# A decoder trunk whose MLP takes its up panels in pairs: seven half products in place of eight, on two thirds of the tokens

## What is computed

```
h2 = (rmsnorm(x, g_norm2[l]) * (1.0 + sc2) + sh2).astype(x.dtype)
ff = jnp.square(jax.nn.relu(h2 @ w_up[l])) @ w_down[l]
x = (x + g2 * ff).astype(x.dtype)
```

## Time and profile before

| what | before |
|---|---|
| median of 3 runs | 2797.01 us |
| lowest and highest | 2795.2 and 2807.06 us |
| profiled execution, first to last instruction | 2801.3 us |
| PE, PEld busy | 97%, 90% |
| DVE, ACT, POOL busy | 44%, 23%, 9% |
| DMA | 295 MB, mean 105 GB/s |

### The profile page before, as it was taken

The page is one execution under the profiler, slowest core; times in us unless marked ns, Lnnn a source line. Parts: engine busy times, 40 slices in busy tenths (PEclk is TensorE's granted clock), DMA queues, the critical chain, the costliest instruction groups (busy, mean ns, idle before and its releaser), DMA issues. The chain is left out here.

```text
span 2801.3 us, 48407 instructions
## 1 busy us (share of the span) xinstructions
PE 2711.2 (97%) x20524; PEld 2531.6 (90%) x20524; DVE 1234.9 (44%) x2205; ACT 644.0 (23%) x1058; POOL 263.6 (9%) x344
## 2 busy tenths in 40 slices
PE   5999989999999999999999999899999999999998
PEld 4999976699999999999989999666999999999998
DVE  5625535557423423324457354456563243242344
ACT  4334324423101101001132442343221000000012
POOL 1101100020000000001111110001100000000010
PEclk9999999999999999999999999899999999999999
DMA  8440159731222221111134101895212111111111
GB/s 310 151 108 31 67 211 328 265 115 40 82 91 85 82 91 58 56 46 46 61 112 118 51 31 62 296 347 214 75 49 79 46 46 50 42 59 46 46 55 69
DMA packets 106873, 295.37 MB, mean 105 GB/s; under 512 B 19605, under 2 KB 32790, under 8 KB 104610
## 3 DMA queue, kind: packets, MB, share of 16 engines
q1 hardware_dynamic: 106498, 291.49, 30.6%
q0 software_dynamic: 160, 0.79, 0.1%
HBM read 269.61 MB, written 22.63 MB: 104 GB/s over the span
## 5 line engine op out<-in xcount | busy, mean ns | idle before, releaser
L307 PE MATMUL PS<-hH,whi 128*128 128x352 f32 x1632 | 533.9, 327 | 8.2 <-DVE hL L2300 6.6
L307 PE MATMUL PS<-hL,whi 128*128 128x352 f32 x1632 | 524.9, 322 | 0.0
L307 PE MATMUL PS<-hH,wlo 128*128 128x352 f32 x1632 | 524.5, 321 | 0.0
L307 PE MATMUL PS<-aH,whi 128*128 128x352 f32 x1344 | 439.9, 327 | 4.0 <-PEq L384 3.5
L307 PE MATMUL PS<-aL,whi 128*128 128x352 f32 x1344 | 432.8, 322 | 0.0
L307 PE MATMUL PS<-aH,wlo 128*128 128x352 f32 x1344 | 432.3, 322 | 0.0
L295 POOL CAST whi<-raw 128x1024 fp32r<-128x1024 f32 x158 | 167.1, 1058 | 1660.1 <-PE PS L307 1332.7
L307 PEld LDWEIGHTS PS<-hH,whi 128*128 128x128 f32 x1632 | 307.4, 188 | 16.9 <-issue 12.7
L307 PEld LDWEIGHTS PS<-hL,whi 128*128 128x128 f32 x1632 | 308.0, 189 | 0.0
L307 PEld LDWEIGHTS PS<-hH,wlo 128*128 128x128 f32 x1632 | 307.3, 188 | 0.0
L853 PE MATMUL PS<-aH,whi 128*128 128x352 f32 x912 | 304.6, 334 | 1.9 <-ACT F L1053 1.9
(11 more groups left out here) (369 smaller groups left out, 3633.7 us busy)
## 6 DMA issues: line engine op xcount, KB each, us to landing
KVp<-kv SPq DMA_DIRECT2D x256, 384.0 KB, 7.2
raw<-w_ff SPq DMA_DIRECT2D x128, 512.0 KB, 3.6
raw<-w_in SPq DMA_DIRECT2D x42, 512.0 KB, 3.6
wad_single<-w_ada SPq DMA_DIRECT2D x40, 512.0 KB, 3.6
wad<-w_ada SPq DMA_DIRECT2D x32, 512.0 KB, 5.6
x_spill<-x SPq DMA_DIRECT2D x2, 4224.0 KB, 14.0
wada<-w_first SPq DMA_DIRECT2D x8, 1024.0 KB, 6.8
raw<-w_out SPq DMA_DIRECT2D x16, 512.0 KB, 4.4
```

The source lines that it names most:

```text
L307: last = nc.tensor.matmul(PS[:, 3 * p + part, 0:CW], w[:, k, :], a[:, k, part * CW:(part + 1) * CW], start=k == 0 and w is wh and a is hig ...
```

## The change

Lines named from here on with order rows are lines of the changed kernel.

**Pairs.** Of 32 up panels a layer, the first four are computed as before. The other 28 go in 14 pairs. For a pair with panels a and b, features in two halves (tiles 0 to 3 and 4 to 7) and the token thirds 0 and 1, the eight half products (2 panels, 2 halves, 2 thirds) are replaced by seven of sums and differences (a scheme of the Strassen kind). The weights come as four quarters, each a half panel of 128 x 512: a0, a1, b0, b1. DVE forms b0 + b1 - a0, a1 less that, b0 + b1, and a0 - b0 (`form_six`, `form_three`, `form_five`, `form_seven`), POOL casts each to its high part, DVE subtracts. On the side of the activations four tensors of 4 tiles by 352 are formed once a layer, in the first group: differences of halves and thirds of h2 (`form_difference`, `form_less`), with a cast on ACT and a subtraction on DVE each. The products land in banks 0 to 3; ACT copies the first to SBUF and DVE combines the rest into the four results (`combine`, each an addition of a bank to SBUF). The third third of tokens is computed as before, in four blocks. A block is 4 tiles by 3 parts, 12 matmuls.

**Pieces.** Each of the pair's six results (2 panels by 3 thirds, 352 columns) goes through ACT in three steps, Relu, Square and Copy to the high part, and through DVE for the low part (`piece_lower`).

**Groups.** There are eight groups of 512 features instead of four of 1024. A down product is then eight half panels of 4 tiles, 36 matmuls each, and their number doubles. DVE adds a half panel to `x` straight from PSUM (`residual_half`), without ACT.

**Weights.** All of these are half panels in four slots (`shi`, `slo`), loaded into four quarter buffers; the SP program is written anew for them.

**Conditions.** Eight condition panels, before beside eight up panels, now stand in the third and fourth panel in five batches and a sixth beside the first down half panel; the 24 of layer 0 that follow stand one each beside the first four down half panels of six groups.

**Last down product.** It still goes by phases, with four tiles to a panel: 12 matmuls for a third instead of 24.

Beside this the change moves constants, lends a part of them as buffers and loads it again at the end of layer 0, and uses some semaphores a second time.

```diff
+                def step(bank, w, k, high_, low_, start, stop):
+                    for a, b_ in ((w[0], high_), (w[0], low_), (w[1], high_)):
+                        last = nc.tensor.matmul(PS[:, bank, 0:CW], a[:, k, :], b_, start=start and a is w[0] and b_ is high_, stop=stop and a is w[1],
+                                                skip_group_check=True)
+                    return last
...
+                def up_pair(p):
+                    b, q, cb = first_unit(p), p - 2, comb_before(p)
...
+                    by_rows(0, w, 0, 0).then_inc(product_done, 1)
...
+                    by_rows(4, w, 0, 2, stop=False).then_inc(eaten, 1)
+                    w = unit(1)
...
+                    by_sums(1, w, 1).then_inc(eaten, 1)
+                    w = unit(2)
...
+                    by_rows(2, w, 1, 1).then_inc(eaten, 1)
+                    w = unit(3)
+                    by_sums(3, w, 0).then_inc(eaten, 1)
+                    w = unit(4)
+                    pe.wait_ge(combined, cb + 1)
+                    by_sums(1, w, 2).then_inc(eaten, 1)
+                    w = unit(5)
+                    pe.wait_ge(combined, cb + 2)
+                    by_sums(2, w, 3).then_inc(product_done, 1)
...
+                    by_rows(5, w, 1, 2, stop=False).then_inc(eaten, 1)
+                    w = unit(6)
+                    pe.wait_ge(taken, 4 * q + 1)
+                    by_rows(0, w, 1, 0, start=False).then_inc(product_done, 1)
+                    by_rows(4, w, 1, 2, start=False).then_inc(eaten, 1)
+                    w = unit(7)
+                    by_rows(5, w, 0, 2, start=False).then_inc(eaten, 1)
...
-                for g in range(FF_GROUPS):
-                    for j in range(0 if g else 2, KT):
-                        panel(pe, s, up(g, j), hH, hL, condition_rows, fold_rows)
...
+                for g in range(GROUPS - 1):
                     for j in range(KT):
...
+                            down_half(g, j)
+                    up_pair(2 * g + 2)
+                    up_pair(2 * g + 3)
+                last_by_phases()
...
+                        act.wait_ge(*((piece_steps, 9 * q + 2 * i + 1) if i < 3 else (taken, 4 * q + i - 1)))
+                        nc.scalar.activation(stage[to], stage[to], ACT.Square).then_inc(piece_steps, 1)
...
+                def form_six(p):
...
+                    link(nc.vector.tensor_tensor(t, quarter[2][:], quarter[3][:], ALU.add))
+                    nc.vector.tensor_tensor(t, t, quarter[0][:], ALU.subtract).then_inc(formed, 1)
...
+                    nc.vector.tensor_tensor(stage[to], stage[a], PS[:, bank, 0:CW], ALU.add).then_inc(combined, 1)
...
+                    nc.vector.scalar_tensor_tensor(xw, PS[:, b0:b0 + 2, 0:CW], mod[:, gate, 0:1], xw, ALU.mult, ALU.add)
...
+                        if g == 0 and j == 0:
+                            form_less(1, 1, 1, 0, 1)
+                            sum_low_half(0, 1)
+                        if g == 0 and j == 1:
+                            form_less(3, 1, 0, 1, 2)
+                            sum_low_half(1, 2)
+                        if g == 0 and j == 2:
+                            form_difference(2, 1, 1, 0, 1)
+                        if g == 0 and j == 3:
+                            sum_low_half(3, 3)
+                            sum_low_half(2, 4)
```

More of the change, by code:

```diff
@@ L375, in trunk @@
     first = len(sems)
+    gathered = [s.num for s in i_g]
+    start_only = [s for s in sems if s.num not in gathered]
+    cleared = (range(sems[0].num, min(gathered)), range(max(gathered) + 1, sems[0].num + first))
+    assert sum(map(len, cleared)) == len(start_only) == first - LAYERS
     i_norm.update(norm("norm1", ROOTS + ("scaled", "modded", "high", "low")))
@@ L738, in _ @@
             def _(sp):
+                if not begun:
+                    for r in cleared:
+                        sp.sem_clear(r)
                 if begun:
@@ L2091, in _ @@
+                if not last_layer:
+                    sp.wait_ge(eaten, CORE)
+                    back = slice(CONST["head"].start + P, CONST["pair"].stop)
+                    sp.dma_start(con[:, back], consts[:, back]).then_inc(con_back, 16)
+                    sp.wait_ge(half_low, CORE + KT)
+                    load(sp, CLASSIC)
+                    load(sp, CLASSIC + 1)
+                    sp.wait_ge(con_back, 16)
+                else:
                     for ph in range(2):
@@ new lines, in by_rows, with by_sums @@
+                def by_rows(bank, w, i, part, start=True, stop=True):
+                    for k in range(HALF):
+                        last = step(bank, w, k, hH[:, HALF * i + k, cut(part)], hL[:, HALF * i + k, cut(part)],
+                                    start and k == 0, stop and k == HALF - 1)
+                    return last
+                def by_sums(bank, w, f):
+                    for k in range(HALF):
+                        last = step(bank, w, k, tH[f][:, k, :], tL[f][:, k, :], k == 0, k == HALF - 1)
+                    return last
@@ new lines, in spread_of, with out_by_phases @@
+                def spread_of(run):
+                    sums, spread = (mid, end)[run][0:2]
+                    pe.wait_ge(N["added"], (KT - 2) * (2 * run + 1))
+                    pe.wait_ge(N["squared"], KT * (2 * run + 1))
+                    pe.wait_ge(s["room"], NCH * START_OF[run] + 2 * KT)
+                    sums(pe, 0)
+                def out_by_phases():
+                    operands = (hH, hL)
+                    ready = lambda part, k: pe.wait_ge(mixed, KT * part + k + 1)
+                    for j, part in [(0, 0), (1, 0), (0, 1), (1, 1)] + [(j, part) for j in range(2, KT) for part in range(2)]:
+                        pe.wait_ge(s["split"], j + 1)
```

703 lines of the change are left out of this document (565 added, 138 removed).

## The result

The changed kernel takes 2785.7 us (median of six executions, 2781.5 to 2786.7), the kernel before 2799.7 (six, 2795.2 to 2807.1). The ratio is 0.9947, with a 95% interval of 0.9933 to 0.9961: **some 15 us faster** (11 to 19). The forecast was 22.7 us less, 2774.3. Measured, 2785.7 lies just above the forecast's own range (2765 to 2785) and inside the one with rivals 1 and 2 (2761 to 2792), and the gain is a third smaller than the sum said.

A forecast was written before the change was run, and what follows sets the result against it. PE, busy for 97% of the span, was taken as the bound. Removed matmuls (-53.5) and the added costs summed to -22.7 us, from 2797.0 to 2774.3; own range 2765 to 2785, with rivals 1 and 2 2761 to 2792.

The forecast's parts named there:

- Rival 1: First group and last product: waits smaller because starts overlap, half of 27 us back, 2761; chance 0.12.
- rival 2: Pairs leak: margin lost to casts and squaring on ACT, some 0.5 us in each of 28, +14, 2788; chance 0.14.
- matmuls removed: Pairs of up panels: 132 matmuls instead of 144, 336 fewer over 28 pairs, 53.5 us less.
- pair in steady state: Pairs: DVE, POOL and ACT keep up with PE, smallest margin 1.4 us, no loss.
- end of a group: Next pair's second block waits for a down residual to free its bank: 2 us in 14 groups (0 to 4).
- differences in the first groups: First group of each layer: forming four differences on DVE delays residuals, PE waits, +13.5 us (7 to 20).
- start: Condition panels beside the last two ordinary panels: a late load costs 0.5 us a layer, 1 us (0 to 4).
- last product, layer 0: Layer 0's last down product: DVE already full, PE's work beside it halved, +10.2 us (8 to 13).
- last product, layer 1: Layer 1's last down product: shorter DVE train, 12.2 of 15.3 us gained, +3.1 us (2 to 6).
- clock: Layer 0's last phase: PE partly idle may drop to the lower clock level, 1 us (0 to 6).
- rival 3: Pairs: DVE becomes the bound through waits for POOL and cast collisions, +70 us, 2844; chance 0.07.
- rival 5: First group: the clock falls to its lower level there too, +22 us a layer, 2818; chance 0.05.

The follow-up runs named there:

- e1: Changed kernel with twelve more matmuls in every pair (28 blocks more), into a bank nobody reads: 2834.1 us, ratio 1.0115 to the kernel before.
- e2: Changed kernel without the four stored differences of tokens, their products reading rows of the input instead; part of the computation left out: 2772.8 us, ratio 0.9889.
- e3: Changed kernel with most operations beside the matmuls cut to 16 columns from the third pair on; part of the computation left out: 2786.0 us, ratio 0.9936.
- e5: Changed kernel with the addresses of weight slots 1 and 2 exchanged and the constants brought back later: 2786.5 us, ratio 0.9950.
- e6: Changed kernel with two halves of weight slots moved out of the lent constants, changing places with two landing quarters: 2778.3 us, ratio 0.9922.
- e4: Changed kernel with layer 0's add of the bias put ahead of the first difference on DVE: 2778.6 us, ratio 0.9918.
- e8: Changed kernel with DVE's residual adds and adds of squares in layer 0's last down product cut to 16 columns: 2780.8 us, ratio 0.9934.

## Why the prediction was right, and where its sum was off

By the forecast's own steps (us against the kernel before, by the trace):

| step | forecast | measured |
|---|---|---|
| matmuls removed | -53.5 | -53.4 (e1: as many put back cost 53.4) |
| pair in steady state | 0 | 0 in waits; **+9.1 in the interval**, with the down panels |
| end of a group | +2 | +2.7 (0.19 x 14) |
| differences in the first groups | +13.5 | +8.9 (e2), with the clock's fall in layer 0 |
| start | +1 | +0.7, a load of conditions in layer 1 |
| last product, layer 0 | +10.2 | +11.1 |
| last product, layer 1 | +3.1 | +3.5 |
| clock | +1 | some 1.4, within the +8.9; else not separate |
| sum | -22.7 | -17 |

The sum can be read directly too. From the first product of the output projection to the next block's first product, layer 0 takes 866.4 us instead of 873.1; from the same place to the end, layer 1 takes 845.4 instead of 855.5. That is 16.8 less.

- **Removed.** Right. e1 is the check from the other side, by its trace.
- **The pair.** The walk through the waits was right: no product waited for weights or combinations, even rival 2's half microsecond was absent, and with a third to a half of the helpers' work gone (e3) 3304 matmuls went through where 3303 had. DVE's collisions with casts exist (a lower half 0.96 at 726.89 in layer 0, where most take 0.69) and cost nothing there. Rivals 2 and 3 fall. Rival 1 came true in part: a third of the first groups' 13.5 was not there, but the last products cost all that was forecast.
- **The step that failed** is the first number of the argument: 0.159 us for a matmul. It was measured in the kernel before and used for the kernel after, as if it belonged to the shape. After the change the mean from one start to the next in the trace is 0.1597 us in the down half panels and 0.1607 to 0.1610 in the pairs behind the stall, against 0.1590 before. That is 0.65 us a group, 9 us in all: as much as the whole error of the forecast. I had bounded every added operation from both sides, and this term, which multiplies 13,000 matmuls, not at all; one part in a hundred of it is 20 us. e3 speaks against contention with the engines, e5 shows that it goes with the weights' address, e6 takes two thirds of it back; the last third is open.
- **First group.** Right in layer 1 in kind (four waits for residuals) and too high in size: 4.0 us of waits against 6.1. (The forecast's 13.5 takes its 2.1 for casts once in each layer, which its text does not say.) In layer 0 the wait was a different one. The text said "a condition (0.23)" and counted its length; it did not ask who waits for it. Behind three operations of the first difference, its bank held PE for 3.3 us, and the clock fell behind that wait. So the 3.8 us of this layer against some 5.2 forecast have another cause than the forecast's. Then the residual waits had no room to appear (e4 brings one back, 1.0 us).
- **Last product.** From the end of the wide phase DVE's train ended at 31.9 us (forecast 31.0; before 36.1); in layer 1 the last residual ended at 22.8 (22.4; before 34.6). The mechanism is DVE, as forecast, but only down to 2.9 us (e8); behind it is ACT.
- **Clock.** The granted clock was 0.81 in layer 0's last stretch, where DVE sets the length, and 1.00 in the first group of layer 1, with waits of up to 1.3 us. In layer 0's first group it fell once, behind the wait of 3.3 (0.66 from 727 to 732). So rival 5 came for a few us of one layer, at some 1.4 us, and not for six half panels of both. The Trainium skill (TensorE: Matmul & The Clock Gate, A second HAM failure mode: psum-queue depth-cycling) warns that micro-idles between groups of matmuls cost clock. The last stretch agrees with it; the four short waits of layer 1's first group cost none.

Two errors with opposite signs, -4.6 in the first group and +9.1 in the interval, leave the forecast some 6 us too good by the trace, 8 by the ratio. The measured terms add up to 17, inside the 11 to 19 of the ratio. That the time came so near is in part luck: with the first group's size right, the forecast would have been 4.6 us lower and further off.

## What to carry to other kernels

Where one engine never idles, the price of its commonest instruction is the term to bound first: a layout change that touches no count can move it by a percent. When a buffer is lent to weights, compare the interval of the matmuls by slot in the trace, from a row that starts behind each block, before looking for waits. And for each small operation that a change leaves behind a long one, ask who waits for its bank: moving one instruction of 0.2 us returned 2.7, and spreading four formations over the blocks that had room returned 8.

## What the hardware showed that I had not expected

The time of a block of 12 matmuls (352 columns) is repeated to a few nanoseconds from group to group in most places, and depends on where its weights lie: in the down half panels of the changed kernel 1.904 to 1.914 us for slots 0 and 1, up to 1.927 for slot 2 and 1.945 for slot 3, whose halves lie in the lent constants and another buffer, and the slower values move when the addresses are exchanged. In its pairs most blocks take 1.92 to 1.94, whatever the slot; in e6 sixteen of the 22 take 1.906 to 1.911. Only behind the stall at a group's end do the times vary between groups: the third block of the first pair takes 1.907 in some and 1.934 in others, with the same addresses. Within a block the starts are 155 to 167 ns apart in a pattern that repeats in most groups. In e2 a block with unchanged operands (the last third's block behind the sixth product) took 1.907 instead of 1.933 when the two blocks ahead of it read other rows, so the address of a block's own operands isn't all of it, as unit 3 of e5 says too. The Trainium skill (TensorE: Matmul & The Clock Gate, Step-by-step: what each phase is for) has two independent read ports and says that loading the next weights takes nothing from the running matmul; read so that the weights' address would not matter either, it does not fit e5 and e6, by up to two parts in a hundred; that the loading itself takes bandwidth isn't shown. Which bits of the address decide stays open; a run with one slot moved in steps would tell. The kernel before, with whole panels in the same buffers, had 159.0 ns throughout the 530 us of the earlier trace rows.
